# Order of the weight fetch in the second MLP product, and order of the split blocks in all pairs and at the change of phase

## The reference, cut to what matters

```
h2 = modulate(x, norm2_w[l], sh2, sc2)
return x + g2 * (jnp.square(jax.nn.relu(h2 @ w_mlp1)) @ w_mlp2)
```

## Time and profile before

| what | us |
|---|---|
| median of 3 runs (lowest, highest) | 1144.76 (1144.01, 1144.79) |
| the profiled execution's own time | 1144.1 |
| its span in the profile | 1142.3 |
| TensorE (PE) busy | 1093.3 (96%) |
| TensorE weight loads (PEld) busy | 866.1 (76%) |
| VectorE busy | 833.2 (73%) |
| ScalarE busy | 507.9 (44%) |
| GpSimd busy | 336.1 (29%) |

### The profile page before, as it was taken

The page is one execution under the profiler, slowest core; times in us unless marked ns, Lnnn a source line. Parts: engine busy times, 40 slices in busy tenths (PEclk is TensorE's granted clock), DMA queues, the critical chain, the costliest instruction groups (busy, mean ns, idle before and its releaser), DMA issues.

```text
span 1142.3 us, 15381 instructions
## 1 busy us (share of the span) xinstructions
PE 1093.3 (96%) x5056; PEld 866.1 (76%) x5056; DVE 833.2 (73%) x1068; ACT 507.9 (44%) x823; POOL 336.1 (29%) x295
## 2 busy tenths in 40 slices
PE   8889999999999899887999999999899999999995
PEld 4468888877888688566888888888687877787783
DVE  3777869636444875799777777777977777687776
ACT  4556523355624222347666666666422122122234
POOL 1000006386202353522323233333322132123233
PEclk9899999999999999899999999999999999999998
DMA  9423241001013673204865757677827745955703
GB/s 370 195 93 100 88 144 38 25 32 38 20 37 129 239 237 132 74 9 155 329 263 225 267 222 264 222 270 272 336 96 273 278 186 198 331 211 187 263 1 147
DMA packets 58894, 199.71 MB, mean 175 GB/s; under 512 B 5600, under 2 KB 6880, under 8 KB 58336
## 3 DMA queue, kind: packets, MB, share of 16 engines
q1 hardware_dynamic: 58848, 199.11, 47.3%
HBM read 139.32 MB, written 59.77 MB: 174 GB/s over the span
## 4 chain that ended last, share of the span: by engine, by line
PE 45%; DMA 3%; DVE 2%; issue 1%; ACT 1%; SPq 0%; POOL 0%; DVEq 0%
PE main L1341 13%; PE ob L1300 13%; PE sm L1300 10%; PE sm L1341 5%; PE ob L1341 3%; DMA raw<-wstream 3%; DVE XR L2435 1%; DVE stage_last L2332 0%; SPq L662 0%; POOL XR L907 0%; DVE stage L2332 0%; DVE XR L2495 0%; ACT slot L1704 0%; DVE t_tmp L2325 0%; DVE hid L2345 0%
## 5 line engine op out<-in xcount | busy, mean ns | idle before, releaser
L1300 PE MATMUL ob<-h_sum,slot 128*128 128x512 f32 x540 | 133.3, 396 | 5.0 <-ACT hid L1747 3.1
L1704 ACT ACTIVATE slot<-raw 128x512 fp32r<-128x512 f32 x80 | 50.4, 631 | 181.0 <-PE main L1341 71.5
L924 PE MATMUL main<-a_hi,w_hi 128*128 128x512 f32 x376 | 125.9, 416 | 2.6 <-DVE a_lo L2138 2.6
L1300 PEld LDWEIGHTS ob<-h_sum,slot 128*128 128x128 f32 x540 | 102.3, 190 | 29.5 <-issue 3.9
L924 PE MATMUL main<-a_lo,w_hi 128*128 128x512 f32 x376 | 116.7, 392 | 0.0
L924 PE MATMUL main<-a_hi,w_lo 128*128 128x512 f32 x376 | 116.2, 390 | 0.0
L2435 DVE SCALAR_TENSOR_TENSOR XR<-main,mods,XR 128x512 f32<-128x512 f32 x112 | 82.8, 747 | 30.8 <-PE main L1341 29.1
L924 PEld LDWEIGHTS main<-a_hi,w_hi 128*128 128x128 f32 x376 | 66.7, 188 | 21.1 <-issue 5.8
L924 PEld LDWEIGHTS main<-a_hi,w_lo 128*128 128x128 f32 x376 | 70.6, 188 | 15.7
L924 PEld LDWEIGHTS main<-a_lo,w_hi 128*128 128x128 f32 x376 | 70.6, 188 | 15.6
L1300 PE MATMUL sm<-h_hi,slot 128*128 128x512 f32 x240 | 79.7, 393 | 0.6 <-ACT hid L1747 0.6
(11 more groups left out here) (334 smaller groups left out, 2508.7 us busy)
## 6 DMA issues: line engine op xcount, KB each, us to landing
hidden_kept<-stage SPq DMA_DIRECT2D x98, 512.0 KB, 4.3
raw<-wstream SPq DMA_DIRECT2D x60, 512.0 KB, 4.0
t_even<-hidden_kept SPq DMA_DIRECT2D x56, 512.0 KB, 4.6
raw<-wstream SPq DMA_DIRECT2D x16, 1024.0 KB, 7.9
stage<-hidden_kept SPq DMA_DIRECT2D x21, 512.0 KB, 3.7
stage_last<-hidden_kept SPq DMA_DIRECT2D x21, 512.0 KB, 4.6
wmod<-wm SPq DMA_DIRECT2D x4, 2048.0 KB, 23.4
mbuf<-wm SPq DMA_DIRECT2D x16, 512.0 KB, 3.9
```

What stands on the lines that cost most here:

```text
L924: ins = pe.matmul(main[:, bank, half * HALF:(half + 1) * HALF], w[:, slot, k, :], x[:, half * HALF:(half + 1) * HALF], start=begin, stop=end)
L1300: ins = pe.matmul(hid_bank(acc, odd), slots1[j][:, w, kp, :], parts[x][:, kp, :], start=PARTS[j][3] and kp == 0 and m == 0, stop=kp == KP ...
L1704: act.activation(slots2[j][:, 0, :, :, :], operand(s, j), ACT.Copy).then_inc(w2_hi, 1)
```

## The change

In SyncE's queue, the fetch of the weights for the first half (s = 0) moves from behind the hidden transfers to in front of them. In chunk 0's part it moves in front of the hidden blocks 4 to 6. In `T_ORDER` blocks 5 and 2 change places, and with it the hand-written order on ScalarE and VectorE in all pairs. At the change of phase VectorE makes the first difference and block 0 before the weight slots, slots 1 and 2 come later and one by one between the t blocks, the two halves of the first read are apart, and the third difference comes after them; ScalarE splits block 1 before slot 2, and block 2 right after the last hidden block.

```
-T_ORDER = (0, 3, 1, 5, 2, 4, 6)
+T_ORDER = (0, 3, 1, 2, 5, 4, 6)
@@ sync: hidden blocks for chunk 1, weights of halves 2 and 3
             for j in range(NPART):
+                if j == 4:
+                    sp.wait_ge(w2_lo, NPART)
+                    load_w2(0, T_MLP + 8, 0)
                 if j in freed:
                     sp.wait_ge(hid_prod, done + freed[j] + 1)
...
-            for s in range(2):
-                sp.wait_ge(w2_lo, (s + 1) * NPART)
-                load_w2(s, T_MLP + 8 + 4 * s, 0)
+            sp.wait_ge(w2_lo, 2 * NPART)
+            load_w2(1, T_MLP + 12, 0)
             def chunk(c, odd, stream):
+                sp.wait_ge(w2_lo, c * (2 * NPART) + NPART)
+                load_w2(0, stream, odd)
                 for j in range(NPART):
                     sp.wait_ge(prod_done, c * (2 * NPROD) + (2 * j + 2))
                     for b in range(2):
                         load_hidden(c, odd, j, b)
-                sp.wait_ge(w2_lo, c * (2 * NPART) + NPART)
-                load_w2(0, stream, odd)
                 sp.wait_ge(w2_lo, c * (2 * NPART) + 2 * NPART)
                 load_w2(1, stream + 4, odd)
@@ scalar, period
                 t_high(prev, old, 1)
+                t_high(prev, old, 2)
+                w1_high(i, 4, odd)
                 t_high(prev, old, 5)
-                w1_high(i, 4, odd)
-                t_high(prev, old, 2)
...
-                if last:
-                    w2_high(0, 0, 2, True)
-                else:
+                if not last:
                     w1_high(i + 1, 1, new)
                 for j in T_ORDER[:2]:
                     t_high(i, odd, j, "last" if last else "")
+                if last:
+                    t_high(i, odd, 1, "last")
+                    w2_high(0, 0, 2, True)
@@ scalar, change of phase
             last_block(NMP - 1, 1)
+            t_high(NMP - 1, 1, 2, "last")
             w2_high(0, 0, 3, True)
-            t_high(NMP - 1, 1, 1, "last")
             t_high(NMP - 1, 1, 5, "last")
-            t_high(NMP - 1, 1, 2, "last")
@@ vector, period
                 w1_low(i, 4, odd)
+                t_low(prev, old, 2)
                 t_made(prev, old, 4)
+                w1_low(i, 5, odd)
                 t_low(prev, old, 5)
-                w1_low(i, 5, odd)
-                t_low(prev, old, 2)
                 w1_low(i, 6, odd)
...
                 if last:
+                    t_made(i, odd, 1)
+                    t_low(i, odd, 0, kind)
                     w2_low(0, 0, 1)
-                    w2_low(0, 0, 2)
+                    t_low(i, odd, 3, kind)
                 else:
                     w1_low(i + 1, 1, new)
-                for j in T_ORDER[:2]:
-                    t_low(i, odd, j, kind)
+                    for j in T_ORDER[:2]:
+                        t_low(i, odd, j)
@@ vector, change of phase
             last_pair = NMP - 1
-            for n in (1, 2, 3):
-                t_made(last_pair, 1, n)
+            t_made(last_pair, 1, 2)
             t_low(last_pair, 1, 1, "last")
+            w2_low(0, 0, 2)
+            dve.wait_ge(x_back[0], 64)
+            read(0, 0, 0, (0,))
+            t_low(last_pair, 1, 2, "last")
+            read(0, 0, 0, (1,))
+            t_made(last_pair, 1, 3)
             w2_low(0, 0, 3)
             t_low(last_pair, 1, 5, "last")
             t_made(last_pair, 1, 4)
-            dve.wait_ge(x_back[0], 64)
-            read(0, 0, 0)
-            t_low(last_pair, 1, 2, "last")
             w2_low(0, 0, 4)
             t_low(last_pair, 1, 4, "last")
+            read(0, 0, 1)
             w2_low(0, 0, 5)
-            read(0, 0, 1)
             t_low(last_pair, 1, 6, "last")
```

## The result

| | before | after |
|---|---|---|
| median, us (lowest to highest) | 1144.76 (1144.01 to 1146.05, 5 runs) | 1137.53 (1135.82 to 1140.53, 5 runs) |
| ratio of the times, 95% interval | | 0.9935 (0.9921 to 0.995) |
| profiled execution, its span | 1144.1, 1142.3 | 1135.82, 1134.0 |

The kernel is 7.2 us faster. 1137.53 lies 2.6 us under the 1140.1 of the forecast, outside its own range (1138.5 to 1141.5) and at the very low end of the wide one (1137.4 to 1142.0). Lines of the kernel from the fetch on are shifted by two (L1341 is now L1343, L881 is L883, L2325 is L2327), and the read by four (L2435 is L2439).

What follows compares the result with a forecast made beforehand. TensorE held 45% of the chain of waits, with VectorE the bound at the change of phase. Fetch -5.3, pairs 0 and change of phase +1.3 gave -4.0, so 1144.1 became 1140.1 us; own range 1138.5 to 1141.5.

Steps and rivals of the forecast that it cites:

- the wide one: Range for the whole kernel's time meant to hold 8 in 10: 1137.4 to 1142.0 us.
- The fetch in chunks 1 to 6: Second product: fetch leaves about 18.6 us earlier, all 5.3 us of stalls go; bounds 4.0 and 5.5.
- The pairs: 13 pairs of the first product, blocks 5 and 2 exchanged: cost 0; without cover, up to 0.6 us a pair.
- The change of phase: Between the products, VectorE the bound: loss of 1.3 us; bounds a gain of 2.4 and a loss of 2.9.
- L881 holds the fourth sum to 813.2: Change of phase: GpSimd's sum blocks VectorE's fourth sum, done 813.8; each such block costs about 1.1 us.
- the gap of 3.3 us: Change of phase: TensorE would wait 3.3 us before sum 3, which needs the read of sum 1.
- the half share of a slow clock: After the gap before sum 3: slow clock makes 1.8 us lost instead of 1.0; 1.3 taken, between the two.
- the gap of 2 to 3 us before sum 3: Change of phase: sign that the forecast is right, TensorE waiting 2 to 3 us before sum 3.
- The walk: Change of phase: VectorE's new queue laid end to end from 803.02, giving starts of sums 0 to 4.
- the change of phase gains too: Rival: GpSimd's sums there fall beside reads or start earlier; gain 0.3 to 2.4, 1136.4 to 1138.5 us; chance 0.14.
- The fetch for chunk 0's second half: Change of phase: waits for slot 6, lands about 830.5, wanted at about 832; cost 0.
- The base: Whole kernel: profiled execution's 1144.1 us as starting value, not the median 1144.76; -4.0 gives 1140.1.

Runs made afterwards that it cites:

- e2: Kernel before with only the weight fetches moved in SyncE's queue, orders unchanged: 1138.18 us, ratio 0.9946.
- e4: Kernel before with only t blocks 5 and 2 exchanged, in all pairs and at the change of phase: 1145.13 us, ratio 1.0009.
- e1: The changed kernel again, unaltered: 1139.0 us, ratio 0.9952.
- e3: Changed kernel with SyncE's old queue back, so only the new orders on ScalarE and VectorE: 1144.21 us, ratio 0.9998.
- e6: Changed kernel with the read of sum 2 directly behind that of sum 1: 1137.9 us, ratio 0.9944.
- e7: Changed kernel with GpSimd's first two sums for chunk 0's second half also waiting for block 5's low part: 1138.28 us, one execution.
- e9: The changed kernel unaltered, third measurement, on a third chip: 1137.44 us, ratio 0.994.
- e11: Changed kernel with the read of sum 1 directly behind the fourth sum, that of sum 2 behind block 4: 1136.41 us, ratio 0.9927.
- e5: Changed kernel with the read of sum 1 behind slot 3, that of sum 2 behind block 4, some slots pushed back: 1136.73 us, ratio 0.9933.
- e8: Kernel before with GpSimd's first two sums for chunk 0's second half also waiting for sum 0's first read: 1145.71 us, one execution.

## Why the prediction was off, point by point

- **The fetch in chunks 1 to 6: right.** -5.3 was forecast, -5.49 measured, and the fetch alone repeats it (e2). The fetch left at 925.19, the stalls went entirely, TensorE became the bound. No hidden block was waited for.
- **The pairs: right.** Cost 0: TensorE is busy 259.30 of 259.41 us in the middle of the first product, and e4 bounds the loss at 2.5 us.
- **The change of phase: mis-sized.** The term was +1.3; it measured -0.13 at chunk 1. The step that failed is "L881 holds the fourth sum to 813.2": the queue was laid out with three operations held, and one was not. Its price, 1.1 us, and with it the gap of 3.3 us and the half share of a slow clock behind it, fell away. So sum 4 came at +18.13 and not at +19.2 or later, and of the signs named as right the gap of 2 to 3 us before sum 3 did not show. The walk was right to 0.2 us for sums 0, 1 and 2. The rival "the change of phase gains too" named the cause rightly (L881 beside reads), but its gain of 0.3 to 2.4 is not there either, because L882 held slot 5. That 1137.53 lies inside this rival's 1136.4 to 1138.5 is luck: what fills the difference lies in earlier stages.
- **The fetch for chunk 0's second half: right.** It left at 815.50 and nothing waited for it.
- **The base.** -4.0 should have been -5.65. That alone makes 1138.5 out of 1144.1. The other 2.65 us are in the profiled execution before the middle of the first product, 1.72 of them in a stage that is the same in both kernels. The 1 us that the median lies under 1138.5 is within the spread of those stages (the last group of the first product began anywhere from 798.75 to 803.27); that it comes from there is argued, since only one of the five executions has a trace. The range's low end allowed for a mis-sized term, and not for this spread on top. The chance of 0.66 on the forecast's own range was too high for so long a walk of dependent steps.

**Open.** Why the same L881 gets in ahead of the fourth sum in the kernel before (also in e2 and e4) and is kept out in the changed one (also in e1, e3, e6, e7, e9, e11), although the two operations ahead of it are slot 3 and block 5 in both (in e4 block 2 in place of block 5), and it starts 0.2 us into the second of them in both (in e7 one operation later). It repeats in every execution, so it is no chance; what decides was not found.

## What to carry to other kernels

When a stall's chain starts with a transfer, look at what stands in front of its issue in the queue, and not at the engines behind it: moving one issue ahead of 14 others gave the whole gain here, 5.5 us in the traces. Where two engines are in each other's way, lay the queue out both ways (first the one held, then the other) and carry both sums; here one operation held or not was 1.1 us and decided between a loss and nothing. A reordering of a stage in which one engine is busy throughout can hand the wait on, in part (e5) or with loss (e8). By the traces it was shortened where reads that TensorE waited for went ahead of low parts that nobody needed yet (1.6 us in e6, 2.2 in e11), but the times do not tell these from the changed kernel.

## What was not expected of the hardware

- A sum of GpSimd that takes 1.3 us took 3.40, 2.81 and 2.22 where two-operand operations of VectorE on SBUF followed each other; each time it ended 1.21 to 1.24 us after VectorE's next read out of PSUM had begun. VectorE's operations beside it took their usual 0.68.
- In other places GpSimd had its turn between two such operations, and the second took 1.78 instead of 0.68.
- Equal gaps of 3.05 us were followed by a granted clock of 1.00 in one execution and 0.50 in another, 3.05 against 4.6 us for 12 matmuls.
